# Per-head bias and mask of a forget-gated attention: from two matmuls per head to GpSimd and the row maximum's own instruction

## The reference, cut to what matters

```python
def fox_attention(q, k, v, f_logit):          # B,S,H,dh = 1,256,8,128
    scale = 1.0 / math.sqrt(dh)
    c = jnp.cumsum(jax.nn.log_sigmoid(f_logit), axis=1).transpose(0, 2, 1)
    ...
        s = jnp.einsum('bhqd,bkhd->bhqk', qi, k32) * scale
        s = s + ci[..., None] - c[:, :, None, :]
        s = jnp.where(kpos[None, :] <= qpos[:, None], s, -jnp.inf)
        p = jax.nn.softmax(s, axis=-1)
        return jnp.einsum('bhqk,bkhd->bqhd', p, v32)
```

## Time and profile before

| What | Before |
|---|---|
| Median of 3 runs | 1051.59 us (1051.52 to 1053.78) |
| The profiled execution's own time | 1051.89 us |
| Its span, first to last instruction | 1050.1 us |
| PE busy | 1043.1 us, 4939 matmuls |
| DVE busy | 754.2 us |
| ACT busy | 598.5 us |
| POOL busy | 84.7 us |
| Mean DMA rate | 231 GB/s |

### The profile page before, as it was taken

The page is one execution under the profiler, slowest core; times in us unless marked ns, Lnnn a source line. Parts: engine busy times, 40 slices in busy tenths (PEclk is TensorE's granted clock), DMA queues, the critical chain, the costliest instruction groups (busy, mean ns, idle before and its releaser), DMA issues.

```text
span 1050.1 us, 12969 instructions
## 1 busy us (share of the span) xinstructions
PE 1043.1 (99%) x4939; PEld 872.3 (83%) x4939; DVE 754.2 (72%) x901; ACT 598.5 (57%) x800; POOL 84.7 (8%) x91
## 2 busy tenths in 40 slices
PE   9999999999999999999999999999999999999997
PEld 7888888888888888888888888888889988888886
DVE  5768777775787675468888978868788666767642
ACT  6573776765385555448784645555366657565531
POOL 1200000000000000000444501400000000000000
PEclk9999999999999999999999999999999999999999
DMA  9945889995487877558867745879976345777741
GB/s 353 400 135 172 298 303 300 294 266 188 184 279 232 244 237 234 199 178 277 250 182 234 242 161 171 249 257 332 312 243 196 115 169 203 242 245 229 244 163 40
DMA packets 97229, 242.84 MB, mean 231 GB/s; under 512 B 15456, under 2 KB 41232, under 8 KB 97040
## 3 DMA queue, kind: packets, MB, share of 16 engines
q1 hardware_dynamic: 92576, 229.42, 67.0%
q0 software_dynamic: 4160, 12.28, 3.4%
q10 hardware_dynamic: 432, 0.33, 0.1%
HBM read 219.43 MB, written 21.50 MB: 229 GB/s over the span
## 4 chain that ended last, share of the span: by engine, by line
PE 98%; DVE 1%; ACT 0%; issue 0%; DVEq 0%
PE ps L823 24%; PE ps L824 24%; PE ps L825 24%; PE ps L862 5%; PE ps L860 5%; PE ps L861 5%; PE ps L957 1%; PE ps L1147 1%; PE ps L1258 1%; PE ps L1257 1%; PE ps L1256 1%; PE ps L1008 1%; PE ps L1009 1%; PE ps L920 1%; PE ps L919 1%; PE ps L918 1%
## 5 line engine op out<-in xcount | busy, mean ns | idle before, releaser
L1967 DVE TENSOR_TENSOR rest<-raw,high 128x2048 fp32r<-128x2048 f32 x129 | 296.2, 2312 | 77.2 <-ACT high L1371 76.6
L823 PE MATMUL ps<-high,xt_high 128*128 128x512 f32 x824 | 324.4, 394 | 0.2 <-DVE rest L1967 0.2
L824 PE MATMUL ps<-rest,xt_high 128*128 128x512 f32 x824 | 320.8, 389 | 0.0
L825 PE MATMUL ps<-high,xt_rest 128*128 128x512 f32 x824 | 320.8, 389 | 0.0
L1371 ACT ACTIVATE high<-raw 128x2048 fp32r<-128x2048 f32 x129 | 244.4, 1911 | 70.1 <-DMA raw<-in_units_dram 66.5
L825 PEld LDWEIGHTS ps<-high,xt_rest 128*128 128x128 f32 x824 | 154.7, 188 | 32.4
L823 PEld LDWEIGHTS ps<-high,xt_high 128*128 128x128 f32 x824 | 154.8, 188 | 32.0 <-DVE rest L1967 0.6
L824 PEld LDWEIGHTS ps<-rest,xt_high 128*128 128x128 f32 x824 | 154.8, 188 | 30.8
L1972 DVE SCALAR_TENSOR_TENSOR rest<-raw,wgain,high 128x512 fp32r<-128x512 f32 x176 | 119.0, 746 | 35.5 <-ACT high L1375 35.5
L1375 ACT ACTIVATE high<-raw,wgain 128x512 fp32r<-128x512 f32 x176 | 110.9, 716 | 9.4 <-DMA raw<-in_units_dram 9.4
L1631 ACT ACTIVATE act<-ps,recips 128x256 f32<-128x256 f32 x44 | 18.5, 471 | 85.0 <-PE ps L825 85.0
(11 more groups left out here) (373 smaller groups left out, 1458.5 us busy)
## 6 DMA issues: line engine op xcount, KB each, us to landing
raw<-in_units_dram SPq DMA_DIRECT2D x350, 512.0 KB, 4.8
gv_turned<-gv_blocked SPq DMA_DIRECT2D x11, 512.0 KB, 5.0
gv_t<-gv_turned SPq DMA_DIRECT2D x44, 128.0 KB, 4.2
turned<-blocked SPq DMA_DIRECT2D x22, 256.0 KB, 5.3
hid_t<-turned SPq DMA_DIRECT2D x88, 64.0 KB, 4.1
fox_turned<-fqT SPq DMA_DIRECT2D x6, 512.0 KB, 3.9
raw<-in_units_dram SPq DMA_DIRECT2D x8, 256.0 KB, 4.8
fqT<-fox_turned SPq DMA_DIRECT2D x16, 128.0 KB, 4.2
```

The source lines that it names most:

```text
L823: pe.matmul(out, sh, wh, start=first, stop=False)
L824: pe.matmul(out, sh, wr, start=False, stop=False)
L825: mm = pe.matmul(out, sr, wh, start=False, stop=last)
L1967: vec.tensor_tensor(rest[:, slot, c], raw[:, slot, c], high[:, slot, c].bitcast(F32), ALU.subtract).then_inc(unit_rest, 1)
```

## The change

1. Bias and mask leave PE. SP stores the eight rows of `fcum` to DRAM (`store_biases`, behind the load of unit 13 of win2; ACT's copy to `hi`, which overwrites `fcum`, waits for the store). GpSimd reads each head's row back, spread to 128 partitions (`spread_bias`), and adds the mask (`mask_bias`), two heads ahead, in three buffers `fbias`. DVE's `tensor_reduce` becomes a `tensor_tensor_reduce`: it adds the bias to the scores in PSUM in place, negates, and takes the minimum, which is the negated maximum. ACT's exponential reads with scale -1. The rounding of the bias (2 ACT, 2 DVE instructions, a memset) goes.
2. GpSimd's 16 DMAs per tile of the recurrence's output are issued in two halves, with a `mask_bias` between them.
3. Memory, tower input and keys are moved as squares within SBUF: 16 DMAs of 32 partitions per tile instead of 1 store and 4 reads. The tower input's are all SP's; of memory and keys SP issues 8 and GpSimd 8 per tile.
4. Probabilities are read back at the top of the next `load`, ahead of the unit's loads, not behind them.
5. DVE prepares units one later from slot 23 on, ACT from slot 26 on (and each again one unit at the end of win2).

```diff
             def load(u):
+                read_probabilities(u - UNIT["win2"] - 33)
...
-                turn_probabilities(u)
+                store_probabilities(u - UNIT["win2"] - 32)
+                store_biases(u)
...
+            def move_squares(queue, dst, src, e, quarters, landed):
+                for q in quarters:
+                    for r in range(4):
+                        queue.dma_start(dst[32 * r:32 * r + 32, q * e:(q + 1) * e], src[32 * q:32 * q + 32, r * e:(r + 1) * e]).then_inc(landed, 16)
...
+            def store_biases(u):
+                if u == UNIT["win2"] + 13:
+                    sync.wait_ge(sem("fcum_ready"), 1)
+                    for c0, w in ((0, P), (P, S)):
+                        sync.dma_start(fcum_dram[:, c0:c0 + w], fcum[0:HH, 0:w]).then_inc(fcum_stored, 16)
...
+            def spread_bias(h):
+                if h == 1:
+                    pool.wait_ge(aux_done, AUX["lv", 1, 128, 0][0] + 1)
+                elif h == HALF + 1:
+                    pool.wait_ge(aux_done, AUX["fs", HALF - 1][0] + 1)
+                elif h:
+                    pool.wait_ge(sem("fox_max"), TT * (h - 1))
+                pool.dma_start(bias_home(h)[:, :], fcum_dram[h].partition_broadcast(P)).then_inc(fbias_landed[h % 2], 16)
+            def mask_bias(h):
+                pool.wait_ge(fbias_landed[h % 2], 16 * (h // 2 + 1))
+                d = bias_home(h)[:, :].rearrange("p (n c) -> p n c", n=3)[:, 0:3:2, :]
+                pool.tensor_tensor(d, d, causal[:, :, :], ALU.add).then_inc(fbias_masked, 1)
...
+                    for h in range(2):
+                        spread_bias(h)
+                    for h in range(2):
+                        mask_bias(h)
+                    for h in range(HH - 2):
+                        spread_bias(h + 2)
+                        if h in (2, 4):
+                            turn_outputs((h - 2) // 2, (0, 1))
+                        mask_bias(h + 2)
+                        if h in (2, 4):
+                            turn_outputs((h - 2) // 2, (2, 3))
+                if name == "mem_post":
...
+                        move_squares(pool, mem[:, tt, :], mem_blocked[:, tt, :], S, (0, 1), oa_turn[2][tt])
+                if name == "ffn2_post":
...
+                        move_squares(pool, mk_turned[:, j, :], mk_blocked[:, j, :], S, (0, 1), oa_turn[2][j])
...
-                    pe.matmul(out[:, 0:P + S], identr[:, n:n + 1].to_broadcast([P, P]), fbias[:, :], start=True, stop=False)
-                    diagonal = out[:, 0:P + S].rearrange("p (n c) -> p n c", n=3)[:, 0:3:2, :]
-                    pe.matmul(diagonal, identb[:, :], causal[:, :, :], start=False, stop=False)
...
-                split_to(UNIT["win2"] + u + 5)
+                split_to(UNIT["win2"] + u + (5 if u < 26 else 4))
...
-                    split_to(UNIT["win2"] + u + (4 if 5 < u < 9 or 20 < u < 23 else 3 if 8 < u < 21 else 5))
+                    split_to(UNIT["win2"] + u + (5 if u < 5 else 3 if 8 < u < 21 else 4))
...
+                        vec.wait_ge(fbias_masked, n + 1)
-                            ins = vec.tensor_reduce(small["negmax"][:, n, tt:tt + 1], src[:, c0:c1], AX_X, ALU.max, negate=True)
+                            vec.tensor_tensor_reduce(src[:, c0:c1], src[:, c0:c1], bias_home(n)[:, c0:c1], -1.0, -3 * NEG,
+                                                     ALU.add, ALU.min, small["negmax"][:, n, tt:tt + 1])\
```

More of the change, by code:

```diff
@@ L366, in build @@
         at_rest = place("at_rest", [P, KC, S], F32R, area)
-        fbias = place("fbias", [P, P + S], F32R, area + 62 * KB)
+        fbias = [place(f"fbias{n}", [P, P + S], F32, area + k * KB) for n, k in enumerate((62, 28, 54))]
         junk_m = place("junk_m", [P, TT, NB], F32, area + 8 * KB)
@@ L399, in build, with keys_blocked @@
         fox_turned = nc.dram_tensor("fox_turned", (8, P, TT * NB), F32, kind="Internal").ap()
[L401 to L405, removed]
+        oa_turn = (sem("oa_blocked"), None, [sem(f"squares_landed{n}") for n in range(2)])
+        mem_turn = (sem("mem_blocked"), [sem(f"mem_turned{n}") for n in range(2)])
+        y2_turn = (sem("y2_blocked"), [sem(f"y2_landed{n}") for n in range(2)])
+        def keys_blocked(j):
+            n, count = taken("mk", j)
+            return pair_taken[n], count
+        def move_squares(queue, dst, src, e, quarters, landed):
+            for q in quarters:
+                for r in range(4):
+                    queue.dma_start(dst[32 * r:32 * r + 32, q * e:(q + 1) * e], src[32 * q:32 * q + 32, r * e:(r + 1) * e]).then_inc(landed, 16)
         def mem_halves(ap, tt, q):
@@ L473, in build, with bias_home @@
         eps_ready = sem("eps_ready")
+        fcum_dram = nc.dram_tensor("fcum_rows", (HH, P + S), F32, kind="Internal").ap()
+        fcum_stored, fbias_masked = sem("fcum_stored"), sem("fbias_masked")
+        fbias_landed = [sem(f"fbias_landed{n}") for n in range(2)]
+        def bias_home(h):
+            return fbias[0 if h % 2 == 0 else 1 + h // HALF]
         fox_blocked, fox_stored = sem("fox_blocked"), sem("fox_stored")
@@ L640, in turn_conv, with read_probabilities @@
                         sync.dma_start(gv_t[32 * r:32 * r + 32, j % 2, :, :], src[r]).then_inc(gv_landed[j % 2], 16)
[L642 to L657, removed]
+            def store_biases(u):
[3 more added lines that the diff above has]
+                        sync.dma_start(fcum_dram[:, c0:c0 + w], fcum[0:HH, 0:w]).then_inc(fcum_stored, 16)
+            def read_probabilities(h):
                 if 0 <= h < HH:
@@ L1741, in _ @@
                     fox_log_sigmoids()
[L1742 to L1745, removed]
                 if u == 5:
@@ L1816, in _ @@
                             c0, c1 = (0, P) if tt == 0 else (P, P + S)
[L1817 removed]
+                            ins = act.activation(fp[:, c0:c1], out[:, c0:c1], ACT.Exp, scale=-1.0,
                                                  bias=small["negmax"][:, n, tt:tt + 1],
@@ L2536, in _ @@
                     vec.wait_ge(aux_taken[AUX["flog", 1][1]], AUX["flog", 1][2] + 1)
-                    step(vec.memset(fbias[:, :].bitcast(F32), 0.0))
                     settle()
```

80 lines of the change are left out of this document (38 added, 42 removed).

## The result

The changed kernel takes 1057.81 us, the median of 6 runs (1055.51 to 1060.14). The old one took 1052.43 us beside it, also in 6 runs. The ratio is 1.0051, with a 95% interval of 1.0039 to 1.0062. The forecast was 1049.2 us, in a range up to 1052.2: the kernel became slower, and by more than any of my rivals put a number on. Of all runs in this document one, of the version with bias and mask alone, fell in the chip's slow state (1157.23 us at a granted clock of 0.85) and is left out.

What follows compares the result with a forecast made beforehand. The prediction took PE as the bound, busy 1043.1 of 1050.1 us. It took 8 x 0.30 = 2.4 us from PE with nothing given back, 1051.6 - 2.4 = 1049.2 us, range 1048.8 to 1052.2.

Steps and rivals of the forecast that it cites:

- Probabilities and biases on SP: SP's queue: read about 1 us earlier, loads held until the store lands with slots in hand; two `fcum` stores cost 0.
- Rival (d): Squares or loads late at mk, wout2 or the last probabilities, landings some 3 us longer; 1050 to 1053 us, chance 0.10.
- Rival (c), POOL's chain: POOL's order becomes the bound at mask 7, behind masks 5, 6 and squares; example 4.8 us late, 1053.6 us; chance 0.15.
- the mask that meets DVE: POOL's mask addition: 0.61 us, or twice that when DVE is on the same memory.
- L: Mean time of POOL's spread biases from issue to landing, taken as 4.7 us; chain 14.2 + 3L, 28.3 us.
- The squares: Memory, at mk: landing 2 us earlier, worth 0 because DVE's order decides; keys earlier, also 0.
- The price of the maxima: DVE's maxima become dearer by p per head, taken as 0.2 us, bounds 0 and 0.4.
- rival (b): Dearer maxima make `at_rest` late at the start of brA; 1050.1 us at p = 0.4, 1051.6 at 0.6; chance 0.22.
- PE's 2.4 us: Bias and mask matmuls leave PE's chain, 0.30 us a head over 8 heads, and nothing fills the gap.
- Rival (e): Scores take 0.96 us a head without the two matmuls as well, so no gain: 1051.6 us; chance 0.05.

Runs made afterwards that it cites:

- the version with bias and mask alone: The changed kernel with the read behind its loads again and without the squares (memory, tower input, keys through DRAM); 1053.41 us, ratio 1.0021.
- the first experiment: The changed kernel with only the probabilities' read moved back behind the loads of its unit; 1051.69 us, ratio 1.0009.
- the new homes: Six places for spread biases instead of three, heads 1 to 3 masked with head 0, 5 and 7 after head 3's scores; ratios 0.9971 to 1.0026.
- The best version: The changed kernel with the probabilities' read back behind its unit's loads, plus the new homes and order on GpSimd; 1049.7 us, ratio 0.9971.
- the version with the store at the top: The changed kernel with the probabilities' store also moved ahead of the unit's loads, SyncE's order read, store, loads; 1050.97 us, ratio 0.9991.
- the last: The best version without the squares: memory, tower input and keys turned through DRAM as in the old kernel; 1052.26 us, ratio 1.0000.

## Why the forecast was wrong, step by step

**The step that failed** stands under "Probabilities and biases on SP": that the read "now holds those loads until the probabilities' store has landed, again with slots in hand". I asked only whether PE waits for the loads. I didn't ask what stands behind the loads in the same queue: the next head's store. I also priced "about 1 us earlier" for the read, while only the first came earlier, and that of head 6 came 11.4 us later (694.37 against 683.00). Nor did the loads have their slots in hand at every engine: ACT waits for them up to 4.2 us in the changed kernel, and in the old kernel with only the read moved this reaches PE as an `at_rest` 0.9 us late. The move turned the order from store, loads, read into read, loads, store, and so put 1 MB in front of the transfer whose landing the whole queue waits for. Shown from both sides: undone, the 7.0 us of waits are gone (1.0009); done alone on the old kernel, 1.0040; the store taken along to the top, 0.9991. Rival (d), 0.10, has the effect and even its size in it: "last probabilities" late, at landings "some 3 us longer". The stores' median went from 2.0 to 5.0 us and the longest from 5.4 to 8.9. But (d) gave no cause for it, and its 1050 to 1053 fell short of 1057.8, for the loop repeats it head after head, and the lower clock came on top. Such a match without its cause is luck.

**Rival (c), POOL's chain,** had 0.15 and is the second cause. Its place and its way through to `at_rest` were right; that its example comes out at 4.8 us late at DVE, against 5.05 measured, is partly chance, as it was made of L = 6.4 and four masks of 1.2 us. Two terms of its sum were too small. One is the mask that meets DVE, which I put at 1.2 us, twice 0.61. In the changed kernel:

```profile
664.36 2.76 POOL L810 TENSOR_TENSOR fbias<-fbias,causal 128x256 f32<-128x256 f32 x1 [5.48 <-DMA fbias<-fcum_rows]
...
671.57 0.68 POOL L810 TENSOR_TENSOR fbias<-fbias,causal 128x256 f32<-128x256 f32 x1
```

And DVE beside the two, a `rest` of two SBUF inputs at the slow one, a scaling of one at the quick one:

```profile
664.29 2.29 DVE L2009 TENSOR_TENSOR rest<-raw,high 128x2048 fp32r<-128x2048 f32 x1
...
671.39 1.02 DVE L2135 TENSOR_SCALAR fp<-fp,expsum 128x128 f32<-128x128 f32 x2
```

The other is L. In the changed kernel the spreads' L is 3.9 us in the median (3.2 to 6.0), under my 4.7, but those of heads 5, 6 and 7 in the first experiment took 6.1, 6.0 and 6.3 us (658.14 to 664.26, 666.89 to 672.93, 679.51 to 685.76). Put into the forecast's sum, 7.9 + 6.6 for the four masks (0.7, 2.6, 2.6, 0.7) + 3.9 + 18.4 for the three spreads is 36.8 us; the chain took 36.9 (649.63 to 686.51), where 28.3 were forecast and 31 were there. Masks and landings have half of the excess each.

**The squares** I put at 0, because "DVE's order decides" at mk and "nobody is late" for the keys. Both were true of the old kernel, at its time of PE. Once PE is some 2.4 us earlier they need not be: without the squares 0.9 us of the gain are taken back at the memory in one profile, and 1.8 us behind the keys in another. But of the two direct comparisons one says 3 us and one says nothing (0.9971 against 1.0000, 0.9983 against 0.9990), and the wait behind the keys occurs once with squares too. So the 0 was set on too little, and what the term is stays open.

**The price of the maxima** was 0.07 us, not 0.2. The pair of one head, beside the earlier trace rows:

```profile
660.77 0.29 DVE L2600 CUSTOM_DVE_ANT_0 ps<-ps,fbias 128x128 f32<-128x128 f32 x1
660.98 0.14 DVE L2600 DVE_READ_ACCUMULATOR2_ANT negmax<- 128x1 f32 x1
660.98 0.47 DVE L2600 CUSTOM_DVE_ANT_0 ps<-ps,fbias 128x256 f32<-128x256 f32 x1
...
661.37 0.42 DVE L2677 COPY fo<-ps 128x256 f32<-128x256 f32 x1
```

The step of the pair is 0.60 us (660.77 to 661.37) against 0.53. The reads of the accumulator are there (a second, left out here, is at 661.37), but each starts together with the instruction behind it and holds nothing up. So rival (b) is out. In the five versions with the new homes the masks are in time and the second `at_rest` keeps PE waiting in no profile; in the best it ends at 689.78, 1.2 us before PE's 691.02.

**PE's 2.4 us** were right, as far as PE goes. The chain at head 0 in the version with the store at the top, beside the earlier trace rows:

```profile
631.41 0.23 PE ps L874
631.64 0.66 PE ps L1230 x4
```

The scores follow the unit's last matmul in one step and still take 0.66 us. By the starts of the same matmuls each of heads 0 to 3 gains 0.33 us and each of heads 4 to 7 0.28 us, 2.4 in all, in this profile and every other without the two. The best version is at 0.9971 of the old one, 3.0 us with an interval of 1.9 to 4.2. Rival (e) is out. My 1049.2 us came near to that version (1049.7), not to this change.

**Open:** why a spread lands in 3.2 us once and 6.3 us another time, which probably makes the two groups of times of the first experiment (the new homes take the upper group away, but they change the order on GpSimd with it); what the squares are worth; and what the later preparation by DVE and ACT (point 5 of the change) and the halved squares (point 2) do by themselves, as they are in every version of the new kernel and no run takes them out.

## What to carry to other kernels

When an issue is moved within a queue, write down the new order of that queue for one whole turn of the loop, and look at every transfer for what now stands directly in front of it: a small transfer on which the queue itself waits must go out before the large ones. When the critical engine is made faster, everything that was just in time for its old pace has to be priced again: a slack that is "set by another engine" in the old trace need not be there in the new one. A change of several parts can hold its gain and its loss in different parts, so time them alone.

## What the runs showed of the hardware that I had not expected

- A GpSimd addition of 128 x 256 took 0.68 us beside a DVE instruction of one SBUF input, and 2.76 us (664.36 to 667.12) when it began 0.07 us behind a `rest` of two (664.29 to 666.58); it ended 0.54 us after that. So did the others that began inside a `rest` in the heads' stretch of the changed kernel and of the first experiment, seven of 1.85 to 2.64 us, each ending 0.52 to 0.54 us after its `rest`. That they stood nearly all the time is an inference from these rows. It can go the other way: at 621.66 the addition of head 0 took 0.69 us in the middle of a `rest`, and that `rest` took 2.99 us instead of 2.29. The Trainium skill, GPSIMD Engine Reference, section Key points, says that GpSimd shares its SBUF interfaces with such DVE instructions; the trace agrees, and shows a short operation made up to four times as long.
- A store of the probabilities, 192 KB, that is issued half a microsecond behind the second of two loads of 512 KB on the same queue lands in 4.9 to 8.9 us, 0.5 to 0.9 us after that load; in front of the loads about 2 us in the median of the old kernel (1.9 to 5.4). The store of the keys, behind two loads in the same way, takes 7.7 us in the old kernel.
- After a standstill of PE of 3.0 us the granted clock was 0.50 and then 0.71 over the next 4 us, and that cost 1.5 us by the starts of the same matmuls; after 5.2 us in the first experiment it was 0.50 for 6 us, 2.3 us, and after 1.8 us in the last 0.50 and 0.78, 1.7 us. The length of the standstill doesn't decide it alone: after waits of 1.1, 1.3 and 1.5 us in the changed kernel, and of 2.0 us for `at_rest` in the version with bias and mask alone, it stayed at 1.00.
